# Two places for a sample's query row, its state and values' row scaled by ScalarE in column blocks, and four small moves in a one-core layer step

## The reference, cut to what matters

```python
def attend_sample(q, k, v, lam, k_past, v_past):         # per sample, k_past: 512 tokens
    s_past = jnp.einsum('bqhcd,bkhcd->bhcqk', q, k_past).astype(F32) * scale
    s_new = jnp.einsum('bqhcd,bkhcd->bhcqk', q, k).astype(F32) * scale
    p = diff_probs(jnp.concatenate([s_past, s_new], axis=-1), lam)
    return (jnp.einsum('bhqk,bkhv->bqhv', p[..., :p_len], v_past) + ...)

def hgrn_steps(q, k, g, v, s0):                          # per sample, one step
    S = jnp.exp(gt)[..., None] * S + kt[..., None] * vt[..., None, :]
    return S, jnp.einsum('bhk,bkhv->bhv', qt, S)

    qa, ka, va, qb, fb, ib, ogb, ga, gb = split_in(xn @ p['w_in'])
    ...
    ya = oa.reshape(b, t, A_V_W) @ p['w_branch_a']
    yb = ob.reshape(b, t, B_V_W) @ p['w_branch_b']
    merged = jax.nn.sigmoid(ga) * ya + jax.nn.sigmoid(gb) * yb
    return merged @ p['w_out'], ka, va, s_new
```

## Time and profile before

| what | value |
|---|---|
| median of 3 runs | 2263.7 us (2262.52 to 2264.01) |
| the profiled execution | 2261.58 us, 1.78 us more than its span |
| its span | 2259.8 us |
| PE busy | 2224.5 us, 98% of the span |
| DVE, ACT, POOL busy | 68%, 50%, 42% |
| mean granted TensorE clock | 0.997 of full |

### The profile page before, as it was taken

The page is one execution under the profiler, slowest core; times in us unless marked ns, Lnnn a source line. Parts: engine busy times, 40 slices in busy tenths (PEclk is TensorE's granted clock), DMA queues, the critical chain, the costliest instruction groups (busy, mean ns, idle before and its releaser), DMA issues. The chain is left out here.

```text
span 2259.8 us, 47757 instructions
## 1 busy us (share of the span) xinstructions
PE 2224.5 (98%) x18881; PEld 2106.5 (93%) x18881; DVE 1544.4 (68%) x2534; ACT 1140.7 (50%) x2343; POOL 955.0 (42%) x1149
## 2 busy tenths in 40 slices
PE   7999999999999999999999999999999999999999
PEld 5899999989999999989887899999999999999999
DVE  5668677777777686776687515416988888876535
ACT  6566666666666666655433402015466666643110
POOL 1135262634444452625443314442155656535431
PEclk9999999999999999999999999999999999999999
DMA  7212122131213131221699713111355454485212
GB/s 301 91 55 94 46 84 66 58 105 56 98 51 103 45 100 48 78 75 40 249 349 344 280 41 122 48 42 59 132 192 188 183 187 180 183 304 198 89 47 94
DMA packets 103513, 288.34 MB, mean 128 GB/s; under 512 B 18426, under 2 KB 26490, under 8 KB 103290
## 3 DMA queue, kind: packets, MB, share of 16 engines
q1 hardware_dynamic: 102138, 281.09, 35.3%
q10 hardware_dynamic: 1152, 4.19, 0.5%
HBM read 213.18 MB, written 63.77 MB: 123 GB/s over the span
## 5 line engine op out<-in xcount | busy, mean ns | idle before, releaser
L172 PE MATMUL h_G<-xn_hi,h_w_hi 128*128 128x344 f32 x1368 | 457.4, 334 | 0.2 <-ACT h_d_oraw L918 0.2
L172 PE MATMUL h_G<-xn_hi,h_w_lo 128*128 128x344 f32 x1368 | 437.0, 319 | 0.0
L172 PE MATMUL h_G<-xn_lo,h_w_hi 128*128 128x344 f32 x1368 | 436.6, 319 | 0.0
L1203 POOL TENSOR_TENSOR h_w_lo<-h_w_raw,h_w_hi 128x1024 fp32r<-128x1024 f32 x58 | 149.2, 2573 | 367.6 <-ACT h_w_hi L780 332.0
L172 PEld LDWEIGHTS h_G<-xn_hi,h_w_hi 128*128 128x128 f32 x1368 | 258.3, 189 | 32.5 <-issue 21.2
L172 PEld LDWEIGHTS h_G<-xn_lo,h_w_hi 128*128 128x128 f32 x1368 | 257.1, 188 | 4.6
L172 PEld LDWEIGHTS h_G<-xn_hi,h_w_lo 128*128 128x128 f32 x1368 | 257.1, 188 | 0.0
L3095 DVE SCALAR_TENSOR_TENSOR x<-t_ps,keep_mod,x 128x344 f32<-128x344 f32 x168 | 94.3, 571 | 163.6 <-PE t_ps L2923 100.9
L2923 PE MATMUL t_ps<-f_act_lo,f_d_hi 128*128 128x344 f32 x528 | 169.4, 321 | 0.0
L2923 PE MATMUL t_ps<-f_act_hi,f_d_lo 128*128 128x344 f32 x528 | 168.8, 320 | 0.0
L2923 PE MATMUL t_ps<-f_act_hi,f_d_hi 128*128 128x344 f32 x528 | 168.5, 319 | 0.1
(11 more groups left out here) (467 smaller groups left out, 6998.1 us busy)
## 6 DMA issues: line engine op xcount, KB each, us to landing
h_w_raw<-in_w_in SPq DMA_DIRECT2D x72, 512.0 KB, 3.7
y_rows<-f_y SPq DMA_DIRECT2D x44, 516.0 KB, 2.7
f_y_pair<-y_rows SPq DMA_DIRECT2D x22, 1032.0 KB, 5.2
h_d_ada_w<-in_w_ada SPq DMA_DIRECT2D x32, 512.0 KB, 4.2
g_kp<-in_cache_k SPq DMA_DIRECT2D x32, 512.0 KB, 6.9
g_vp<-in_cache_v SPq DMA_DIRECT2D x32, 512.0 KB, 5.5
f_a<-in_w_ffn SPq DMA_DIRECT2D x57, 256.0 KB, 2.6
h_w_raw<-in_w_mix SPq DMA_DIRECT2D x24, 512.0 KB, 3.5
```

The lines of the kernel that those rows point to most:

```text
L172: ins = eng.matmul(out, w[:, k * P:(k + 1) * P], x[:, k, columns], start=(k == 0 and n == 0), stop=(k == n_k - 1 and n == 2))
L1203: pool.tensor_tensor(wlo[w][:, :], raw[r][:, :], whi[w][:, :].bitcast(F32), ALU.subtract).then_inc(lo_done.sem, 1)
```

## The change

1. **Norm:** ACT's `split(2)` moves from behind row 4 of the input to behind row 1.
2. **Heads:** PE's wait for `ones_ready` moves behind `late_value(2)`. In the last head PE's two transposes of the samples' rows (L1171) and ACT's copy of them move behind that chunk's matmul piece.
3. **Gates, the query row:** it gets two places, `qB[0]` as before and `qB[1]` in the last gate tile, which is not written until later. Row 1 is loaded at the start of the stage; the row of i + 2 is loaded once the keys of i are multiplied, behind the keys of i + 1.
4. **Gates, the state:** `next_state(i)` waits for `st_out(i - 1)` and `state_out(i - 1)` and loads the state of i. It moves from behind `st_new(i - 1)` and the values' row, ahead of the pages of values, to behind these pages and the first two pages of keys that follow.
5. **Gates, the scaling:** ACT's new `scale_state(i)`, directly behind the exponent, scales `st` (8 blocks of 128 columns) and `vB` (8 more), each block by its own factor per partition. DVE's two multiplications over 1024 columns go; its sum waits for all 16. DVE's order becomes: cuts of gate tiles, copy of the turned weights, sum, keys.
6. **Gates to tail:** row 0 of the branch input is split (ACT 3 x 344 columns, DVE 3 x 344) at the end of the gates stage, once all of `oa` is back and PE is past the first k of its last piece (`row_free`); the tail begins with row 1. Ln and Exp of gate tile 10 move from the end of the gates stage into the tail.

The core of the diff (the same replacement of `qB` by `qB[i % 2]` in POOL's and DVE's `keys` is left out, as is the removal in the tail of row 0's own branch):

```diff
@@ norm, ACT
                 act.activation(hi[:, k, :], x[:, k, :], ACT.Copy).then_inc(high.sem, 1)
+                if k == 1:
+                    split(2)
...
-                if k == KT // 2:
-                    split(2)
@@ gates
-        qB, vB = row("qB"), row("vB")
+        qB, vB = [row("qB"), gate[1][:, H - 1, 0:D]], row("vB")
@@ gates, SP
             load_pages(0)
+            load_spread(1)
+            def next_state(i):
+                sp.wait_ge(st_out.sem, st_out.at(i - 1, 1))
+                sp.wait_ge(rec_out.sem, rec_out.at(i - 1, 1))
+                load_state(i)
             for i in range(NS):
                 for j in range(PAGES):
+                    if i and j == 2:
+                        next_state(i)
                     sp.wait_ge(k_summed.sem, k_summed.at(i, j + 1))
                     if i + 1 < NS:
-                        if j == 2:
-                            sp.wait_ge(k_scaled.sem, k_scaled.at(i, 2))
-                            load_spread(i + 1)
                         load_keys(i + 1, j)
+                if i + 2 < NS:
+                    sp.wait_ge(k_scaled.sem, k_scaled.at(i, 2))
+                    load_spread(i + 2)
...
                     load_values(i + 1)
-                if i + 1 < NS:
-                    sp.wait_ge(st_out.sem, st_out.at(i, 1))
-                    sp.wait_ge(rec_out.sem, rec_out.at(i, 1))
-                    load_state(i + 1)
                 sp.wait_ge(pv.sem, pv.at(i, 1))
                 if i + 1 < NS:
                     load_pages(i + 1)
@@ gates, ACT
+            def scale_state(i):
+                for rows, factor, loaded in ((st, c["s_f"], st_in), (vB, c["s_kk"], vb_in)):
+                    act.wait_ge(loaded.sem, loaded.at(i, 1))
+                    for b in range(NS):
+                        block = rows[:, b * P:(b + 1) * P]
+                        act.activation(block, block, ACT.Copy, scale=factor[:, i, b:b + 1]).then_inc(st_scaled.sem, 1)
...
                     act.activation(sc[:, :], sc[:, :], ACT.Exp, bias=sv[:, 1:2], scale=SCALE, accum_out=sv[:, 2:3]).then_inc(s_exp.sem, 1)
+                    scale_state(i)
...
+                    act.wait_ge(oa_in.sem, oa_in.at(KT, 0))
+                    act.wait_ge(row_free.sem, 1)
+                    for j in range(NP):
+                        if j == NP - 1:
+                            act.wait_ge(samples_in.sem, 1)
+                        act.activation(oh[:, 0, cols(j)], x1[:, 0, cols(j)], ACT.Copy).then_inc(row_hi.sem, 1)
-                    for t in range(cut_tiles(NS - 1).stop, N_TILES - 1):
+                    for t in range(cut_tiles(NS - 1).stop, N_TILES - 2):
                         finish_tile(t)
@@ gates, DVE
-                dve.wait_ge(st_in.sem, st_in.at(i, 1))
-                ch(dve.tensor_tensor(st3, st3, head(sf, i), ALU.mult))
                 if i == IN_SET:
                     select(i - 1)
...
-                dve.wait_ge(vb_in.sem, vb_in.at(i, 1))
-                ch(dve.tensor_tensor(vB3, vB3, head(skk, i), ALU.mult))
-                ch.sync()
-                dve.tensor_tensor(st[:, :], st[:, :], vB, ALU.add).then_inc(st_new.sem, 1)
...
                     cut(gate_tile(m)).then_inc(gate_cut.sem, 1)
+                dve.wait_ge(p_turned.sem, p_turned.at(i, 1))
+                dve.tensor_copy(pt[:, :], Y[:, 0:PAGES * QUAD]).then_inc(p_read.sem, 1)
+                ch.sync()
+                dve.wait_ge(st_scaled.sem, st_scaled.at(i, 2 * NS))
+                dve.tensor_tensor(st[:, :], st[:, :], vB, ALU.add).then_inc(st_new.sem, 1)
                 if i + 1 < NS:
                     keys(i + 1)
```

More of the change, by code:

```diff
@@ L163, in __call__, with product @@
         return t
-def product(eng, out, whi, wlo, xhi, xlo, n_k, columns, between=None):
+def product(eng, out, whi, wlo, xhi, xlo, n_k, columns, between=None, first=None):
     for k in range(n_k):
@@ L173, in product @@
                              start=(k == 0 and n == 0), stop=(k == n_k - 1 and n == 2))
+        if k == 0 and first is not None:
+            ins.then_inc(first.sem, 1)
     return ins
@@ L995, in _ @@
                         piece(h, n)
+                    if k == 1 and no_next(h):
+                        act.wait_ge(rows_turned.sem, 1)
+                        act.activation(rows[:, :, :], X[0:H * NS, 0, 0:2 * P].rearrange("p (a b) -> p a b", a=2), ACT.Copy).then_inc(rows_ready.sem, 1)
                     act.wait_ge(os_done.sem, os_done.at(h, k + 1))
@@ L1531, with gates_stage @@
 IN_SET = NS // SETS
-def gates_stage(nc, a, o, c, d, xh, xl, gate, slots, x1, third):
+def gates_stage(nc, a, o, c, d, xh, xl, gate, slots, x1, third, oh, ol):
     with Stage(c) as ctx:
@@ L2002, in _ @@
             ch(dve.tensor_tensor(ob, ob, c["s_og"][:, :, :].rearrange("p a b -> p (a b)"), ALU.mult))
+            for j in range(NP):
+                dve.wait_ge(row_hi.sem, j + 1)
+                ch(dve.tensor_tensor(ol[:, 0, cols(j)], x1[:, 0, cols(j)], oh[:, 0, cols(j)].bitcast(F32), ALU.subtract))
             ch.sync()
@@ L2544, in high @@
             def high(n):
[L2545 removed]
+                for k in range(n == 0, KT):
                     branch_in(act, n, k)
[L2547 to L2554 removed]
+                    act.activation(oh[:, k, :], x[:, k, :], ACT.Copy).then_inc(o_hi.sem, 1)
+            for sig, n in ((first_hi, NP - 1), (o_hi, 1)):
+                act.sem_inc(sig.sem, n)
             high(0)
[L2557 removed]
             act.wait_ge(gate_cut.sem, 1)
[L2559 to L2561 removed]
+            for half in gate:
+                g = half[:, H - 1, :]
+                ch(act.activation(g, g, ACT.Ln))
+                ch.sync()
+                act.activation(g, g, ACT.Exp, scale=-1.0).then_inc(gate_ready.sem, 1)
             def square(t):
@@ L2807, in by_tiles @@
                     for j in range(NP):
[L2808 to L2811 removed]
+                        if n is not None and j == 0:
                             pe.wait_ge(o_hi.sem, o_hi.at(n * KT + k + 1, 0))
@@ L3149, in norm @@
                         rest(j, k - 1)
-            low(0, range(KT))
+            for sig, n in ((first_lo, NP - 1), (o_lo, 1)):
+                dve.sem_inc(sig.sem, n)
+            low(0, range(1, KT))
             dve.wait_ge(o_lo.sem, KT)
```

87 lines of the change are left out of this document (27 added, 60 removed).

## The result

| | before | changed |
|---|---|---|
| median of 6 runs | 2263.43 us (2260.97 to 2264.01) | 2281.7 us (2280.32 to 2283.42) |
| span of the profiled execution | 2259.8 us | 2281.6 us |
| PE busy, gates stage | 174.0 of 184.5 us | 182.4 of 206.8 us |

What follows compares the result with a forecast made beforehand. PE, busy 98%, was taken to bound the kernel. New gates waits of 20, less the old 8.4, plus 0.5 of low clock gave about +12; with -3.2 of small moves, 2270.4 profiled, 2272.5 median, range 2256 to 2284 us.

Steps and rivals of the forecast that it cites:

- Mechanism: Gates: PE's waits go from the sums to the state's product, 1 to 4 us at nearly every sample; ACT idles for the state.
- One sign that I had named: Gates: turns of samples 2 and 5 wait 3 us or more.
- the price of a round: Gates, state's round trip: 20.6 us against 19.3 that PE needs, 1.3 more per sample, 8 for samples 2 to 7.
- The landing: Gates: the state lands +13.9 us behind `st_new` of the sample before, between +11.4 and +14.7.
- my far end of 22.6: Gates: longest round considered, 14.7 + 5.0 + 1.2 + 1.5 + 0.2 = 22.6 us, 3.3 more per sample.
- The small moves: Norm, transposes and tail (parts 1, 2, 6): together -3.2 us (0 to -6.3).
- The low clock: Gates: 1.6 us lost before; behind two or three longer waits now, but a slower PE eats its own wait; +0.5.
- The two late samples: Gates, samples 1 and 4: ACT's split comes late, delaying POOL and SP; 4.5 us each (2 to 5.5), 9 in all.
- The first round: Gates: sample 0's state goes out late behind `finish_early` and the scalings; PE waits 2.9 us for sample 1's state.
- My 1.6 for the tail: Tail: PE's first product waited 1.96 us and a low clock followed; -1.6 us (0 to -3.6).
- The third rival: Gates: the loop at its far end, 22.6 us for six samples, +19, giving 2282.7 us; chance 0.16.
- The rival on the other side: Gates: the state lands in time, query-row waits go, only two late POOL turns remain; 2253.5 us; chance 0.14.

## Why the prediction was right in kind and half in size

**Mechanism: right.** The waits went to the state's product, ACT stood for the state's landing ahead of its scalings, VectorE no longer waited for a query row, and the place of one load on SP undoes 22.6 us. One sign that I had named did not come: the turns of samples 2 and 5 waited 0.64 and 1.51, not 3 or more; the state's products of these samples waited instead, 4.27 and 3.70.

**The step that failed: the price of a round.** I added waits to PE's rounds: 2.9, six times 1.3, and twice 4.5. Two terms of the round were mis-sized. The landing was taken at +13.9 and was at +16.1 in sample 3's round (the end I had given was 14.7). The first page went out 1.1 us behind the values' row and not 0.5: it does so with ACT's issue elsewhere too, and the earlier trace rows already had 1.13 between the state and the first page. The seven transfers from that page to the state took 14.9 us and not 12.8: the second page went out 2.3 behind the first instead of 1.1, as ACT issues the way out at that moment, and that transfer is in the queue as well. The scalings took 4.8, not 4.3: eight of 128 columns in 2.45 is 0.30 each. Together that is 2.7 us; the sum beside POOL and the hand-overs were as taken. 23.3 is beyond my far end of 22.6.

**A slip in the same step.** I gave the last round the same 1.3 as the others, but its turn is three pieces behind the one before, so PE needs some 3.8 us less there (24 matmuls 0.157 apart), about 15.5 and not 19.3; a round of 20.6 waits about 5. It was 19.8 in fact. By my terms the seven rounds between the state's products should have been added as 22.2, 25.1, 20.6, 20.6, 25.1, 20.6 and 20.6, which is 154.8 us. Between the products at 1119.30 and 1284.12 lie 164.8: 22.8, 27.0, 23.3, 22.2, 26.6, 23.2 and 19.8. (Between the sums it is 166.7, as PE came to the first product 1.9 us behind its sum.) The gates stage was 10.3 us longer than forecast: about 4 are this slip, most of the rest is the price of the rounds. (The small moves gave 2.7 less than forecast. The profiled execution, 2283.4, was thus 13.0 over my 2270.4; the medians are only 9.2 apart, as this execution lay 1.7 above its median, where I had counted 2.1 below.) Where a loop around one buffer is longer than the engine's work, the sum is made over the rounds, and not over what each exceeds the engine's work by.

**The low clock: no loss of its own.** I took +0.5 and PE busy grew by 8.3. But the round holds nothing of PE, so a slower PE between two sums waits that much less at the next, as the prediction said; the 8.3 and the 14.0 of idle are two parts of one sum. That is argued from the rows of the round and was not tried.

**The two late samples: right, sized too large** (9 against 5.6 when undone; the rounds of 27.0 and 26.6 against 23.3).

**The first round:** a wait of 3.34 at the place I named (2.9 predicted). What it is worth by itself stays open: the run made for it did not bring the state earlier.

**The small moves: right** (-3.2 predicted, -3 to -4 alone). In the changed kernel norm gave -0.6 at the gates' start. At the tail the wait of 1.96 became two:

```profile
1298.45 0.40 PE L2828 MATMUL t_ps<-branch_hi,h_w_hi 128*128 128x344 f32 x1 [1.04 <-DVEq L3156]
1300.79 0.40 PE L2828 MATMUL t_ps<-branch_hi,h_w_hi 128*128 128x344 f32 x1 [0.70 <-DVE branch_lo L3072]
```

From the tail's first product to the end the changed kernel takes 983.2 us and the kernel before 983.1, though the granted clock behind the first product was 0.52 for 3.5 us before and 1.00 now. The two waits add up to 1.74 us. Twenty us on PE was 4 matmuls (0.6 us) ahead of the kernel before, and in the last 283 us it stood 0.6 us more; what it waited for there was not traced. My 1.6 for the tail did not come in this kernel.

**The third rival** (2282.7, chance 0.16) named the time within 1 us of 2281.7. It is the same loop at its far end, and the rounds did lie near its 22.6. The agreement to 1 us is in part luck: it too has the slip in the last round, and it took the late turns at 5 beside it.

**The rival on the other side** (2253.5) priced the query row's wait at all of 10 us. Behind that cause stand others: pages of keys, POOL's products, and the short last round. No run's median came below 2255.6.

**The better version.** The small moves and the second place for the query row, with the state loaded ahead of the pages and VectorE scaling in its old order: 2256.5 and 2257.0, 0.27% below the kernel before (ratio 0.9973, 0.9963 to 0.9982).

## What to carry to other kernels

Before a load is moved back, follow its one buffer round: out, free, in, scaled, used. Count to the landing and not to the issue: what lies ahead of the load in the queue is part of the round. If that round comes near the period of the engine that bounds, every us by which it exceeds what stands next counts in every pass, and work that was free on another engine is no longer free. And a wait that is removed is worth only the distance from it to the next one; ask what stands behind it, and what an earlier arrival will collide with.

## What the runs showed of the hardware

- VectorE and GpSimd beside each other on SBUF: a cut of 128 x 1032 took 2.8 to 2.9 us instead of 0.69, a product of 128 x 1024 up to 3.40 instead of 1.23, and the loss was so large that transfers arriving earlier made the kernel 10.5 us slower. The Trainium skill, page "SBUF — State Buffer", section "Who interferes with whom", names the port pair that both share. It says that VectorE contends with GpSimd in its two-port modes, and with two inputs in SBUF where GpSimd reads SBUF, and that whichever comes second is fully blocked. The longer durations here agree with that; no run shows the ports themselves.
- Two engines that issue transfers at the same moment: SP's four pages took 4.80 us to issue where ACT issued a state at that time, and 3.64 where it did not.
- The clock: behind waits of 3.34 and 4.27 us the granted clock was 0.50 for the next 3.4 and 3.5 us, at 1142.0 and 1169.0 in the rows above, that is 1.2 GHz. Behind the 2.44 at 1271.37 it stayed at 1.00.
- A queue: the same 512 KB of a state landed 3.5 to 3.7 us behind their issue with little ahead of them, and 7.8 behind six pages and the way out of the old state.
